# Dilated attention in a six-layer single-core kernel: the head norms' squares as high and low part, the key norms behind the next queries, and the group shares worked out over 128 rows

## The chip, the cores and the metric

One Trainium2 chip, one of its cores. The metric is the time of one execution on the device, in microseconds (us).

## The reference

A token stream of 512 positions by 1024 features goes through four layers (a mixer and a gated feed-forward each) and one more mixer. The third layer's mixer is dilated attention, and the change lies in it alone. It has three groups of 16 heads, each head 64 wide, with dilations 1, 4 and 16. Cut to what matters:

```python
qkv = (h @ w_qkv).reshape(b, s, 3, 3, 16, 64)
for g, (window, dil) in enumerate(((128, 1), (512, 4), (2048, 16))):
    q = head_rms_norm(qkv[:, :, g, 0], q_gain[g])      # each head's 64 numbers
    k = head_rms_norm(qkv[:, :, g, 1], k_gain[g])
    v = qkv[:, :, g, 2]
    o, l = dilated_group_attention(q, k, v, bias_g, dil, 64)   # softmax within the group; l = log of its sum
wts = softmax(stack(lses), axis=0)                     # the share of each group, per head and position
o = einsum('gbsh,gbshe->bshe', wts, stack(outs))
return o.reshape(b, s, 1024) @ w_o
```

## The kernel before

Bass code with one in-order program for each engine, written out by Python loops; every wait is on a semaphore count (`K.at(event)`). Features lie on partitions, the 512 positions on the free axis. A weight matrix comes in units of 128x2048 numbers (`raw`), which ScalarE rounds to fp32r (`wh`, `high`) and VectorE completes with the rest (`wl`, `low`). A product with a weight tile is three fp32r matmuls: high by high, high by low, low by high (`gemm`). Plain fp32 operands are used elsewhere; the trace shows an fp32 matmul as two records.

**The attention stage** (`attention_tensor` at L1845 and its sisters for the other engines) goes over three groups g, and in each over ten steps c. Step c of 0 to 7 makes the queries (j=0) and keys (j=1) of head pair c: 24 matmuls each, into a PSUM bank of the ring `K.gb` (four banks). The norm of each needs the sum of squares over a head's 64 rows: ScalarE squares the bank into `sq`, `head_tensor` (L1664) multiplies `sq` by a block matrix of ones (`K.bones`, in `cst`) in one fp32 matmul, and `head_scalar` (L1671) takes Ln and Exp of the result into `htf`. `head_vector` (L1680) multiplies the bank by gain and `htf` into `qk`. Step c also does the scores of pair c-1 (`scores_tensor`, L1690), and for pair c-2 the transposes of the probabilities `Pm` (`products_tensor`, L1766), their copies to SBUF (`PT`, `turned_out`: ScalarE the even ones, VectorE the odd ones), and the products with the values. The norms, transposes and scores share the ring `K.mb` of four banks: a bank is taken again only when its reader is done. For c of 2 to 7 the key norm's matmul stands behind the second transpose of `products_tensor`:

```python
        m.then_inc(*pe.up("T", t))
        if n == 1 and c + 2 < 8:
            head_tensor(K, pe, g, c + 2, 1)
```

Steps 8 and 9 have no projection of their own: they finish the last two pairs, and in groups 0 and 1 make the values of the next group. `mst` and `den` keep each row's maximum and sum of exponentials, 128 rows by group, block and head. Each pair's output goes through `os` to DRAM (`sA`).

**The mix** (`mix_tensor` at L1960 and its sisters) behind it has every engine wait for the end of the attention on all engines (`fence`, L237) and for the last two writes to `sA`. TensorE turns `mst` and `den` to 16 rows (heads) by 512 positions in 24 transposes; VectorE works out the three shares on those 16 rows, six copies and a chain of twelve operations of 512 columns and a reciprocal, with three Exp on ScalarE between; they end in `M`, which GpSimd has set to zero first (`mset`, L2081). Then, for each of 8 pairs c, three fp32 matmuls with a selection matrix `sel` spread a head's share over its 64 rows, VectorE and GpSimd multiply the three outputs `ol` (read back from `sA` by `mix_sync`, L2092, into three buffers) by them and add, ScalarE and GpSimd make the fp32r high and low parts (`omh`, `oml`), and TensorE's `take_in` multiplies them with the output weights.

## Time and profile before

| | us |
|---|---|
| median of 3 runs (lowest, highest) | 3106.11 (3103.87, 3107.86) |
| the profiled execution | 3106.0 |
| its span in the trace | 3104.2 |
| TensorE busy | 2840.2 (91%) |
| VectorE, ScalarE, GpSimd busy | 1560.2, 1092.7, 236.4 |
| mean granted clock of TensorE | 0.955 |

Busy time is summed over the span. The trace's matmuls are pipelined, so a record of 0.39 us may stand every 0.23 us; what a stream of matmuls costs is read from the starts. The granted clock is 1.00 at TensorE's full 2.4 GHz and 0.50 at 1.2 GHz. The attention stage's pair loops lie between 1200 and 1731 us of the span, the mix between 1731 and about 1830.

### The profile page before, as it was taken

The page shows a single profiled execution, that of the slowest core. Times are in us where ns is not written, and L with a number is a line of the kernel's source. Part 1 is how long each engine was busy: PE and PEld are TensorE (multiplying, and loading weights), DVE is VectorE, ACT ScalarE, POOL GpSimd, SP SyncE. Part 2 cuts the span into 40 slices and gives each one's busy share as a digit, 9 for nine tenths or more (in the row PEclk, how much of TensorE's full clock was granted, in tenths as well). Part 3 has the DMA queues.
Part 4 walks back from the last instruction along what each step waited for, and adds up shares of the span by engine and source line. Part 5 has one row for each costly group of instructions (what it writes and reads, how often), then busy time and mean ns, then how long its engine had stood idle before and what let it go on. Part 6 is the DMA issues. An engine that isn't in the chain of part 4 may idle for free.

```text
span 3104.2 us, 37866 instructions
## 1 busy us (share of the span) xinstructions
PE 2840.2 (91%) x15334; PEld 2271.0 (73%) x15334; DVE 1560.2 (50%) x2305; ACT 1092.7 (35%) x1672; POOL 236.4 (8%) x215
## 2 busy tenths in 40 slices
PE   5999997579999989989999699999799999888887
PEld 5787886467888867767777478888688888666665
DVE  5776663844434433553424554344554344544665
ACT  4332332353222223544536242122332122442342
...
GB/s 110 85 144 172 144 164 175 201 145 94 132 116 123 100 61 95 69 76 94 70 101 85 121 87 95 95 99 95 52 86 103 97 95 95 78 42 42 40 15 43
DMA packets 115135, 305.32 MB, mean 98 GB/s; under 512 B 28064, under 2 KB 73568, under 8 KB 86160
## 3 DMA queue, kind: packets, MB, share of 16 engines
...
q8 instruction: 120, 1.97, 0.3%
...
## 4 chain that ended last, share of the span: by engine, by line
PE 79%; DVE 8%; ACT 4%; issue 3%; POOL 1%; SPq 1%; DMA 0%; ACTq 0%; DVEq 0%; POOLq 0%
PE ps L94 78%; DVE s_ L121 2%; PE ps L99 1%; ACT htf_ L117 1%; ACT wh_ L117 1%; SPq L158 1%; DVE H_ L121 1%; DVE htf_ L135 1%; ACT hh_ L117 1%; ACT sq_ L117 0%; DVE R_ L121 0%; DVE ol_ L121 0%; DVE x_ L121 0%; ACT rs_ L117 0%; POOL hl_ L121 0%
## 5 line engine op out<-in xcount | busy, mean ns | idle before, releaser
L94 PE MATMUL ps<-hh_,wh_ 128*128 128x512 f32 x2184 | 872.9, 400 | 19.0 <-DVE hl_ L121 11.5
L94 PE MATMUL ps<-hl_,wh_ 128*128 128x512 f32 x2184 | 857.8, 393 | 0.0
L94 PE MATMUL ps<-hh_,wl_ 128*128 128x512 f32 x2184 | 857.2, 392 | 0.0
L121 DVE TENSOR_TENSOR wl_<-raw_,wh_ 128x2048 fp32r<-128x2048 f32 (+2 forms) x213 | 480.8, 2257 | 556.8 <-ACT wh_ L117 556.7
L117 ACT ACTIVATE wh_<-raw_ 128x2048 fp32r<-128x2048 f32 (+2 forms) x213 | 399.8, 1877 | 374.9 <-PE ps L94 356.7
L94 PEld LDWEIGHTS ps<-hh_,wh_ 128*128 128x128 f32 x2184 | 414.3, 190 | 121.7 <-issue 10.5
L94 PEld LDWEIGHTS ps<-hh_,wl_ 128*128 128x128 f32 x2184 | 414.4, 190 | 88.0
L94 PEld LDWEIGHTS ps<-hl_,wh_ 128*128 128x128 f32 x2184 | 415.0, 190 | 87.2 <-issue 3.5
L94 PE MATMUL ps<-ah_,wl_ 128*128 128x512 f32 x704 | 279.5, 397 | 0.0
L94 PE MATMUL ps<-ah_,wh_ 128*128 128x512 f32 x704 | 278.3, 395 | 0.0
L94 PE MATMUL ps<-al_,wh_ 128*128 128x512 f32 x704 | 277.7, 395 | 0.0
L117 ACT ACTIVATE sg_<-sg_ 128x512 f32<-128x512 f32 x88 | 55.7, 633 | 305.3 <-DVE sg_ L121 305.3
L94 PEld LDWEIGHTS ps<-al_,wh_ 128*128 128x128 f32 x704 | 132.1, 188 | 32.7
L94 PEld LDWEIGHTS ps<-ah_,wh_ 128*128 128x128 f32 x704 | 132.1, 188 | 32.5 <-issue 1.3
L94 PEld LDWEIGHTS ps<-ah_,wl_ 128*128 128x128 f32 x704 | 132.1, 188 | 31.5
L121 DVE TENSOR_TENSOR sg_<-sg_,ps 128x512 f32<-128x512 f32 x88 | 60.5, 688 | 171.2 <-PE ps L94 130.4
L117 ACT ACTIVATE ah_<-sg_ 128x512 fp32r<-128x512 f32 x88 | 55.7, 633 | 238.9 <-DVE sg_ L121 238.9
L121 DVE TENSOR_TENSOR x_<-x_,ps 128x512 f32<-128x512 f32 x104 | 71.2, 684 | 127.2 <-PE ps L94 127.2
L117 ACT ACTIVATE sq_<-x_ 128x512 f32<-128x512 f32 x70 | 44.2, 632 | 217.7 <-DVE x_ L121 209.7
L94 PE MATMUL ps<-wh_,hh_ 128*128 128x512 f32 (+2 forms) x272 | 104.3, 383 | 9.6 <-POOL hl_ L121 5.8
L94 PE MATMUL ps<-wl_,hh_ 128*128 128x512 f32 (+2 forms) x272 | 102.3, 376 | 0.0
L94 PE MATMUL ps<-wh_,hl_ 128*128 128x512 f32 (+2 forms) x272 | 102.2, 376 | 0.0
...
## 6 DMA issues: line engine op xcount, KB each, us to landing
...
```

The source lines that it names most:

```text
L94: return self.e.matmul(out, lhsT, rhs, start=start, stop=stop, skip_group_check=True)
L99: return self.e.transpose(out, a, ident)
L117: return self.e.activation(out, a, f, bias=bias, scale=scale)
L121: return Nothing() if self.e is None else self.e.tensor_tensor(out, a, b, op)
L135: return self.e.scalar_tensor_tensor(out=out, in0=a, scalar=s, in1=b, op0=op0, op1=op1)
L158: return Nothing() if self.e is None else self.e.dma_start(out, a)
```

## The change

- The squares are split by ScalarE into `sqh` (fp32r) and, by GpSimd, the rest `sql`; `head_tensor` multiplies each by an fp32r copy of the ones (`bonr`), two fp32r matmuls in the place of one of fp32. There is one `sqh` and one `sql` for both j, so each is written only when the matmul before has read it.
- The key norm of pair c-1 is taken between the query and key projections of step c; that of the last pair in `products` of step 7.
- Group 0's `mst` and `den` are brought into the other groups' order of positions at steps 3 and 5 of group 1 (`regroup`, 8 transposes each time, a copy each on ScalarE and VectorE).
- The shares are worked out before they are turned, over 128 rows by 64 columns a group: maxima at group 2's steps 1 and 8, one Exp in step 9, the rest in step 9 behind the last `PT` copy. Then 12 transposes turn them, ScalarE and VectorE split them into `Mh` and `Ml` (16 rows), and 48 fp32r matmuls replace the 24 of fp32. `M`, its memset and the 512 KB load of `sel` are gone; 16x16 of `sel` are loaded early and spread by VectorE.
- The fences before the mix no longer name the last writes to `sA`; the loads of pairs 6 and 7 wait for them.

```diff
 def head_tensor(K, pe, g, c, j):
     b = K.mb.take("n", g, c, j)
     pe.wait_ge(*K.after(pe, K.mb, "n", g, c, j))
-    pe.wait_ge(*K.at("a.sq", g, c, j))
-    pe.mm(b, K.bones, K.sq[j][:, :], True, True).then_inc(*pe.up("n", g, c, j))
+    A = K.att
+    pe.wait_ge(*K.at("a.ones"))
+    pe.wait_ge(*K.at("a.sqh", g, c, j))
+    pe.mm(b, A.ones[:, :], A.sqh[:, :], True, False)
+    pe.wait_ge(*K.at("a.sql", g, c, j))
+    pe.mm(b, A.ones[:, :], A.sql[:, :], False, True).then_inc(*pe.up("n", g, c, j))
+
+
+def squares_scalar(K, ac, g, c, j):
+
+    ac.wait_ge(*K.at("qk", g, c, j))
+    if c or g:
+        ac.wait_ge(*K.at("a.sql", *((g, c - 1) if c else (g - 1, 7)), j))
+    ac.act(K.sq[j][:, :], K.gb["qk", g, c, j], ACT.Square).then_inc(*ac.up())
+    if j:
+        ac.wait_ge(*K.at("n", g, c, 0))
+    elif c or g:
+        ac.wait_ge(*K.at("n", *((g, c - 1) if c else (g - 1, 7)), 1))
+    ac.wait_ge(*ac.now())
+    ac.act(K.att.sqh[:, :], K.sq[j][:, :], ACT.Copy).then_inc(*ac.up("a.sqh", g, c, j))
+
+
+def squares_gpsimd(K, po, g, c, j):
+    po.wait_ge(*K.at("a.sqh", g, c, j))
+    po.tt(K.att.sql[:, :], K.sq[j][:, :], K.att.sqh[:, :].bitcast(F32), ALU.subtract).then_inc(*po.up("a.sql", g, c, j))
 ...
         for y, (x, c0, nk, _) in enumerate(sub):
             m = pe.tr(b[0:nk, 128 * y:128 * y + 128], A.Pm[i][:, h, x, c0:c0 + nk], K.ident)
         m.then_inc(*pe.up("T", t))
-        if n == 1 and c + 2 < 8:
-            head_tensor(K, pe, g, c + 2, 1)
     pe.mark("a.T", g, c)
     for n in range(0, len(todo), 2):
         if scores is not None:
             scores_tensor(K, pe, g, scores, n // 2)
+        if n == 0 and c == 5:
+            head_tensor(K, pe, g, 7, 1)
         weigh(n)
     pe.mark("O", g, c)
 
@@ -1826,8 +1852,11 @@
     for n in range(len(turned_parts(g))):
         if turned_number(g, c, n) % 2 == 0:
             turned_out(K, ac, g, c, n)
-        if n == 1 and c + 2 < 8:
-            head_scalar(K, ac, g, c + 2, 1)
+    if c == 5:
+        head_scalar(K, ac, g, 7, 1)
+    if (g, c) == (2, 7):
+        ac.wait_ge(*K.at("m.e"))
+        ac.act(K.att.E[:, :, :], K.att.E[:, :, :], ACT.Exp).then_inc(*ac.up("m.x"))
     ac.wait_ge(*K.at("O", g, c))
     if 8 * g + c > 1:
         ac.wait_ge(*K.at("a.sA", 8 * g + c - 2))
@@ -1838,8 +1867,81 @@
     for n in range(len(turned_parts(g))):
         if turned_number(g, c, n) % 2:
             turned_out(K, dv, g, c, n)
-        if n == 1 and c + 2 < 8:
-            head_vector(K, dv, g, c + 2, 1)
+    if c == 5:
+        head_vector(K, dv, g, 7, 1)
+
 ...
+def regroup_tensor(K, pe, back):
+    A = K.att
+    for n, src in enumerate(statistics(K)):
+        b = K.mb.take("rg", back, n)
+        pe.wait_ge(*K.after(pe, K.mb, "rg", back, n))
+        if not back:
+            pe.wait_ge(*K.at("a.P", 0, 7, 1))
+            pe.wait_ge(*K.at("a.mx", 0, 7, 1))
+            for x in range(4):
+                m = pe.tr(b[0:16, 128 * x:128 * x + 128], src[:, 0, x, :], K.ident)
+        else:
+            pe.wait_ge(*K.at("out", "rg", 0, n))
+            for r in range(4):
+                m = pe.tr(b[:, 16 * r:16 * r + 16], A.turn[:, n, :].rearrange("p (i r) -> p r i", r=4)[:, r, :], K.ident[0:16, 0:16])
+        m.then_inc(*pe.up("rg", back, n))
+
+
 ...
+def shares_vector(K, dv, part):
+    A = K.att
+    mst, den = (t[:, :, :, :].rearrange("p g b x -> p g (b x)") for t in statistics(K))
+    E, F, Q = A.E, A.F, A.Q
+    if part == 0:
+        dv.wait_ge(*dv.now())
+        for n in range(2):
+            dv.wait_ge(*K.at("rg", 1, n))
+        dv.tt(Q[:, 0, :], mst[:, 0, :], mst[:, 1, :], ALU.max).then_inc(*dv.up())
+    elif part == 1:
+        dv.wait_ge(*dv.now())
+        dv.tt(Q[:, 0, :], Q[:, 0, :], mst[:, 2, :], ALU.max).then_inc(*dv.up())
+        dv.wait_ge(*dv.now())
+        dv.tt(E[:, :, :], mst, Q[:, 0:1, :].broadcast_to([128, 3, 64]), ALU.subtract).then_inc(*dv.up("m.e"))
+    else:
+        dv.wait_ge(*K.at("a.P", 2, 7, 1))
+        dv.wait_ge(*K.at("out", "rg", 1, 1))
+        dv.wait_ge(*K.at("m.x"))
+        dv.tt(F[:, :, :], E[:, :, :], den, ALU.mult).then_inc(*dv.up())
+        dv.wait_ge(*dv.now())
+        dv.tt(Q[:, 0, :], F[:, 0, :], F[:, 1, :], ALU.add).then_inc(*dv.up())
+        dv.wait_ge(*dv.now())
+        dv.tt(Q[:, 0, :], Q[:, 0, :], F[:, 2, :], ALU.add).then_inc(*dv.up())
+        dv.wait_ge(*dv.now())
+        dv.recip(Q[:, 1, :], Q[:, 0, :]).then_inc(*dv.up())
+        dv.wait_ge(*dv.now())
+        dv.tt(F[:, :, :], E[:, :, :], Q[:, 1:2, :].broadcast_to([128, 3, 64]), ALU.mult).then_inc(*dv.up("m.F"))
+        dv.wait_ge(*K.at("m.sel"))
+        dv.cp(K.mix.sel[:, :, :].rearrange("p c (n x) -> p (c n) x", n=2),
+              A.sel0[:, :].rearrange("p (n x) -> p n x", x=1).broadcast_to([16, 16, 64])).then_inc(*dv.up("m.selr"))
 ...
                     pe.wait_ge(*K.after(pe, K.gb, "qk", g, c, j))
                     gemm(K, pe, K.gb["qk", g, c, j], rhs, 8)
                     pe.mark("qk", g, c, j)
+                    if c and not j:
+                        head_tensor(K, pe, g, c - 1, 1)
                 head_tensor(K, pe, g, c, 0)
             if c > 1:
                 products_tensor(K, pe, g, c - 2, c - 1 if c < 9 else None)
+            if g == 1 and c in (3, 5):
+                regroup_tensor(K, pe, c // 4)
             if c > 7 and g < 2:
                 values_tensor(K, pe, g + 1, c - 8)
-            if c < 2:
-                head_tensor(K, pe, g, c, 1)
             if c == 1:
                 scores_tensor(K, pe, g, 0)
 ...
             if c < 8:
                 for j in range(2):
                     highs(K, ac, 8)
-                    ac.wait_ge(*K.at("qk", g, c, j))
-                    if c or g:
-                        ac.wait_ge(*K.at("n", *((g, c - 1) if c else (g - 1, 7)), j))
-                    ac.act(K.sq[j][:, :], K.gb["qk", g, c, j], ACT.Square).then_inc(*ac.up("a.sq", g, c, j))
+                    squares_scalar(K, ac, g, c, j)
+                    if c and not j:
+                        head_scalar(K, ac, g, c - 1, 1)
                 head_scalar(K, ac, g, c, 0)
 ...
+            if g == 2 and c in (1, 8, 9):
+                shares_vector(K, dv, c - 7 if c > 7 else 0)
 ...
     A = K.mix
-    for n, (src, name) in enumerate(((K.att.mst, "M"), (K.att.den, "dn"))):
-        for g in range(3):
-            b = K.mb.take("m.t", n, g)
-            pe.wait_ge(*K.after(pe, K.mb, "m.t", n, g))
-            for x in range(4):
-                m = pe.tr(b[0:16, 128 * x:128 * x + 128], src[:, g, x, :], K.ident)
-            m.then_inc(*pe.up("m.t", n, g))
+    for g in (2, 0, 1):
+        b = K.mb.take("m.t", g)
+        pe.wait_ge(*K.after(pe, K.mb, "m.t", g))
+        pe.wait_ge(*K.at("m.F"))
+        for x in range(4):
+            m = pe.tr(b[0:16, 128 * x:128 * x + 128], K.att.F[:, g, 16 * x:16 * x + 16], K.ident)
+        m.then_inc(*pe.up("m.t", g))
 ...
-            pe.wait_ge(*K.at("m.F"))
-            pe.wait_ge(*K.at("m.sel"))
-            pe.mm(b, A.sel[:, c, :], A.M[:, g, :], True, True).then_inc(*pe.up("m.b", c, g))
+            pe.wait_ge(*K.at("out", "m.t", g))
+            pe.wait_ge(*K.at("m.selr"))
+            pe.mm(b, A.sel[:, c, :], A.Mh[:, g, :], True, False)
+            pe.mm(b, A.sel[:, c, :], A.Ml[:, g, :], False, True).then_inc(*pe.up("m.b", c, g))
 ...
+def shares_high(K, ac, g):
+
+    ac.wait_ge(*K.at("m.t", g))
+    ac.act(natural(1, K.mix.Mh[:, g, :], False), natural(1, K.mb["m.t", g][0:16, :], True), ACT.Copy).then_inc(*ac.up("m.Mh", g))
+
+
+def shares_low(K, dv, g):
+
+    dv.wait_ge(*K.at("m.Mh", g))
+    dv.tt(natural(1, K.mix.Ml[:, g, :], False), natural(1, K.mb["m.t", g][0:16, :], True),
+          natural(1, K.mix.Mh[:, g, :].bitcast(F32), False), ALU.subtract).then_inc(*dv.up("out", "m.t", g))
+
+
 ...
     A = K.mix
-    M, E, Q, dn = A.M[0:16, :, :], A.E, A.Q, A.dn
-    dv.wait_ge(*K.at("m.z"))
-    for n, dst in enumerate((M, dn)):
-        for g in range(3):
-            dv.wait_ge(*K.at("m.t", n, g))
-            dv.cp(natural(g, dst[:, g, :], False), natural(g, K.mb["m.t", n, g][0:16, :], True)).then_inc(*dv.up("out", "m.t", n, g))
-    dv.wait_ge(*dv.now())
-    dv.tt(Q[:, 0, :], M[:, 0, :], M[:, 1, :], ALU.max).then_inc(*dv.up())
-    dv.wait_ge(*dv.now())
-    dv.tt(Q[:, 0, :], Q[:, 0, :], M[:, 2, :], ALU.max).then_inc(*dv.up())
-    dv.wait_ge(*dv.now())
-    for g in range(3):
-        dv.tt(E[:, g, :], M[:, g, :], Q[:, 0, :], ALU.subtract).then_inc(*dv.up("m.e", g))
-    for g in range(3):
-        dv.wait_ge(*K.at("m.x", g))
-        dv.tt(E[:, g, :], M[:, g, :], dn[:, g, :], ALU.mult).then_inc(*dv.up())
-    dv.wait_ge(*dv.now())
-    dv.tt(Q[:, 1, :], E[:, 0, :], E[:, 1, :], ALU.add).then_inc(*dv.up())
-    dv.wait_ge(*dv.now())
-    dv.tt(Q[:, 1, :], Q[:, 1, :], E[:, 2, :], ALU.add).then_inc(*dv.up())
-    dv.wait_ge(*dv.now())
-    dv.recip(Q[:, 0, :], Q[:, 1, :]).then_inc(*dv.up())
-    dv.wait_ge(*dv.now())
-    for g in range(3):
-        dv.tt(M[:, g, :], M[:, g, :], Q[:, 0, :], ALU.mult).then_inc(*dv.up())
-    dv.mark("m.F")
+    for g in (2, 0, 1):
+        shares_low(K, dv, g)
 ...
 
 def mix_sync(K, sp):
     A, d = K.mix, K.d
-    sp.dma(A.sel[:, :, :], d["sel"]).then_inc(*K.lane("sel").up("m.sel"))
-    sp.wait_ge(*K.at("a.sA", 22))
-    sp.wait_ge(*K.at("a.sA", 23))
     for c in range(8):
         if c > 2:
             sp.wait_ge(*K.at("m.l", c - 3))
+        if c > 5:
+            sp.wait_ge(*K.at("a.sA", 16 + c))
         for g in range(3):
```

ScalarE's order in group 1, one step (`sq0`, `sq1` the squares of queries and keys, `htf` Ln and Exp of a norm, `PT` a transposed block, `os` the output). Before:

```order
L117 ACTIVATE sq0_<-ps0 128x512 [waits scalar_done,tensor_done]
L117 ACTIVATE sq1_<-ps1 128x512 [waits scalar_done,tensor_done]
L117 ACTIVATE htf0_<-ps6,eps_ 128x512 [waits scalar_done,tensor_done]
L117 ACTIVATE htf0_<-htf0_ 128x512 [waits scalar_done]
L117 ACTIVATE PT0_<-ps7 128x512 [waits tensor_done]
L117 ACTIVATE htf1_<-ps5,eps_ 128x512 [waits scalar_done,tensor_done]
L117 ACTIVATE htf1_<-htf1_ 128x512 [waits scalar_done]
L117 ACTIVATE os0_<-ps2 128x512 [waits sA0,tensor_done]
```

and in the changed kernel:

```order
L117 ACTIVATE sq0_<-ps0 128x512 [waits scalar_done,gpsimd_done,tensor_done]
L117 ACTIVATE sqh_<-sq0_ 128x512 [waits scalar_done,tensor_done]
L117 ACTIVATE htf1_<-ps7,eps_ 128x512
L117 ACTIVATE htf1_<-htf1_ 128x512 [waits scalar_done]
L117 ACTIVATE sq1_<-ps1 128x512 [waits gpsimd_done,tensor_done]
L117 ACTIVATE sqh_<-sq1_ 128x512 [waits scalar_done,tensor_done]
L117 ACTIVATE htf0_<-ps4,eps_ 128x512
L117 ACTIVATE htf0_<-htf0_ 128x512 [waits scalar_done]
L117 ACTIVATE PT0_<-ps5 128x512 [waits tensor_done]
L117 ACTIVATE os0_<-ps2 128x512 [waits scalar_done,sA0,tensor_done]
```

The keys' Ln and Exp (`htf1`) went from behind the transposed block to ahead of the keys' squares, and a rounding to `sqh` now stands between the keys' squares and the queries' Ln.

TensorE's order in the changed kernel, where a step's key projection (`ps3`) begins and ends:

```order
L94 MATMUL ps5<-sqh_,bonr_ 128x512 [waits scalar_done]
L94 MATMUL ps5<-sql_,bonr_ 128x512 [waits gpsimd_done]
L94 MATMUL ps3<-hh_,wh0_ 128x512
L94 MATMUL ps3<-hl_,wh0_ 128x512
L94 MATMUL ps3<-hh_,wl0_ 128x512
...
L94 MATMUL ps6<-sqh_,bonr_ 128x512 [waits scalar_done]
L94 MATMUL ps6<-sql_,bonr_ 128x512 [waits gpsimd_done]
L99 MATMUL ps7<-cst_,Pm0_ 128x128 [waits vector_done]
```

The pair into `ps5` is the norm of the step before's keys, the pair into `ps6` that of this step's queries; before, only the latter stood here, as one fp32 matmul.

VectorE's order at the end of the attention, from the last block's statistics to the mix, before:

```order
L128 TENSOR_SCALAR nmx_<-nmx_ 128x4 [waits vector_done]
L139 COPY PT3_<-ps7 128x512 [waits tensor_done]
L139 COPY M_<-ps4 16x512 [waits sA0,sA1,gpsimd_done,vector_done,tensor_done,scalar_done]
L139 COPY M_<-ps5 16x512 [waits tensor_done]
```

and in the changed kernel (`V_` here holds the shares in work):

```order
L128 TENSOR_SCALAR nmx_<-nmx_ 128x4 [waits vector_done]
L121 TENSOR_TENSOR V_<-V_,mst_ 128x64 [waits vector_done]
L121 TENSOR_TENSOR V_<-mst_,V_ 128x192 [waits vector_done]
L139 COPY PT3_<-ps7 128x512 [waits tensor_done]
L121 TENSOR_TENSOR V_<-V_,den_ 128x192 [waits vector_done,scalar_done]
L121 TENSOR_TENSOR V_<-V_ 128x64 [waits vector_done] x2
L151 RECIPROCAL V_<-V_ 128x64 [waits vector_done]
L121 TENSOR_TENSOR V_<-V_ 128x192 [waits vector_done]
L139 CAST sel_<-sel0_ 16x1024 [waits sel]
L121 TENSOR_TENSOR Ml_<-ps4,Mh_ 16x512 [waits gpsimd_done,vector_done,scalar_done,tensor_done]
```

The chain of operations that stood behind the fence stands ahead of it, on 64 or 192 columns; behind the fence three subtractions are left.

## Rows read from the trace of the kernel before

**Rows 1.** The page, the chain that ended last, by engine.

```profile
PE 79%; DVE 8%; ACT 4%; issue 3%; POOL 1%; SPq 1%; DMA 0%; ACTq 0%; DVEq 0%; POOLq 0%
```

**Rows 2.** Timeline of one step of group 1: start us, us, engine, operation.

```profile
1463.27 0.39 PE L94 MATMUL ps<-hh_,wl_ 128*128 128x512 f32 x1
1463.50 1.02 PE L94 MATMUL ps<-sq_,cst_ 128*128 128x512 f32 x2
1463.70 0.60 ACT L117 ACTIVATE sq_<-ps 128x512 f32<-128x512 f32 x1 [4.01 <-PE ps L94]
1464.36 1.04 PE L99 MATMUL ps<-cst_,Pm_ 128*128 128x128 f32 x8
1464.56 0.69 ACT L117 ACTIVATE htf_<-ps,eps_ 128x512 f32<-128x512 f32 x1 [0.26 <-PE ps L94]
1465.23 1.02 PE L94 MATMUL ps<-sq_,cst_ 128*128 128x512 f32 x2
1465.81 0.58 ACT L117 ACTIVATE PT_<-ps 128x512 f32<-128x512 f32 x1
1465.94 0.75 DVE L135 SCALAR_TENSOR_TENSOR qk_<-ps,gq_,htf_ 128x512 f32<-128x512 f32 x1 [4.41 <-ACT htf_ L117]
1466.54 1.16 PE L94 MATMUL ps<-qk_ 64*128 64x128 f32 x16 [0.28 <-ACT PT_ L117]
1466.61 0.68 DVE L139 COPY PT_<-ps 128x512 f32<-128x512 f32 x1
1467.63 1.09 PE L94 MATMUL ps<-PT_,V_ 128*64 128x128 f32 x16
```

**Rows 3.** The chain, group 1 from its first step: start us, us, what.

```profile
1385.62 62.74 PE ps L94 x298
1450.37 14.16 PE ps L94 x82
```

**Rows 4.** The chain, group 0's step 7.

```profile
1330.11 0.70 ACT htf_ L117
...
1332.95 3.21 PE ps L94 x32
...
1336.16 0.68 DVE Pm_ L121
```

**Rows 5.** The chain, group 2's steps 7 and 8.

```profile
1711.08 0.70 ACT htf_ L117
...
1718.40 1.11 PE ps L99 x4
```

**Rows 6.** GpSimd's operations of the mix by tile: ns min/median/max, first and last start.

```profile
L121 POOL TENSOR_TENSOR ol_<-ol_,sq_ x8: 1266/1509/2868, 1754.0 to 1791.8; 128x512 f32<-128x512 f32 x8
```

**Rows 7.** Timeline from the last products to the first use of the shares.

```profile
1728.87 1.97 PE L94 MATMUL ps<-PT_,V_ 128*64 128x128 f32 x16 [0.87 <-DVE PT_ L139]
...
1731.94 0.37 SPq L158 DMA_DIRECT2D sel_<-in_sel  x1
...
1733.69 4.30 SPq L158 DMA_DIRECT2D ol_<-sA  x9
...
1745.62 3.34 DVE L151 RECIPROCAL Q__<-Q__ 16x512 f32<-16x512 f32 x1
...
1756.64 0.69 DVE L121 TENSOR_TENSOR ol_<-ol_,ps 128x512 f32<-128x512 f32 x1 [0.96 <-PE ps L94]
```

**Rows 8.** The tile of the outputs read back, its transfers.

```profile
DMA to landing us min/median/max: 2.6/3.8/5.9
```

**Rows 9.** The chain in the mix, VectorE's last sum of two pairs in succession.

```profile
1779.02 0.70 DVE ol_ L121
...
1783.52 0.70 DVE ol_ L121
```

**Rows 10.** Windows behind TensorE's waits: the number behind GpSimd's busy time is the clock.

```profile
1364.00:1366.00 2.00, 2.00 (x7) 1.58 (x6) 1.97 (x7) 0.00 (x0) 0.00 (x0) 0.55 0.00 0
...
2729.00:2731.00 2.00, 0.42 (x5) 0.42 (x5) 2.00 (x4) 1.38 (x3) 0.00 (x0) 1.00 0.42 78
```

More of the change, by code:

```diff
@@ L155, in mset, with dma @@
         return Nothing() if self.e is None else self.e.memset(out, v)
-    def dma(self, out, a):
-        return Nothing() if self.e is None else self.e.dma_start(out, a)
+    def dma(self, out, a, single=False):
+        if self.e is None:
+            return Nothing()
+        return self.e.dma_start(out, a, allow_slow_non_contiguous=True) if single else self.e.dma_start(out, a)
 class Lane:
@@ new lines, in regroup_scalar, with regroup_vector @@
+def regroup_scalar(K, ac, back):
+    ac.wait_ge(*K.at("rg", back, 1))
+    if not back:
+        ac.wait_ge(*K.at("O", 0, 7))
+        ac.act(K.att.turn[:, 1, :], K.mb["rg", 0, 1][0:16, :], ACT.Copy).then_inc(*ac.up("out", "rg", 0, 1))
+    else:
+        ac.act(K.att.den[:, 0, :, :].rearrange("p b x -> p (b x)"), K.mb["rg", 1, 1][:, 0:64], ACT.Copy).then_inc(*ac.up("out", "rg", 1, 1))
+def regroup_vector(K, dv, back):
+    dv.wait_ge(*K.at("rg", back, 0))
+    if not back:
+        dv.wait_ge(*K.at("O", 0, 7))
+        dv.cp(K.att.turn[:, 0, :], K.mb["rg", 0, 0][0:16, :]).then_inc(*dv.up("out", "rg", 0, 0))
+    else:
+        dv.cp(K.att.mst[:, 0, :, :].rearrange("p b x -> p (b x)"), K.mb["rg", 1, 0][:, 0:64]).then_inc(*dv.up("out", "rg", 1, 0))
@@ L1872, in attention_scalar @@
     A = K.att
+    ac.act(A.ones[:, :], K.bones, ACT.Copy).then_inc(*ac.up("a.ones"))
     rstd_scalar(K, ac, 4)
@@ L1891, in attention_scalar @@
                 products_scalar(K, ac, g, c - 2)
+            if g == 1 and c in (3, 5):
+                regroup_scalar(K, ac, c // 4)
             if c == 8 and g == 0:
                 residues_scalar(K, ac, range(4, 8))
-            if c < 2:
-                head_scalar(K, ac, g, c, 1)
             if 0 < c < 9:
@@ L1914, in attention_vector @@
                 lows(K, dv, 16)
+                if c:
+                    head_vector(K, dv, g, c - 1, 1)
                 head_vector(K, dv, g, c, 0)
@@ L1919, in attention_vector @@
                 products_vector(K, dv, g, c - 2)
+            if g == 1 and c in (3, 5):
+                regroup_vector(K, dv, c // 4)
             if c == 8 and g == 0:
                 residues_vector(K, dv, g_, range(4, 8))
-            if c < 2:
-                head_vector(K, dv, g, c, 1)
             if 0 < c < 9:
@@ L1933, in attention_gpsimd @@
         norm_gpsimd(K, po, 4, k)
-    residues_gpsimd(K, po)
+    for g in range(3):
+        for c in range(8):
+            for j in range(2):
+                squares_gpsimd(K, po, g, c, j)
+        if g == 0:
+            residues_gpsimd(K, po)
     po.mark("end", "po", "attend")
@@ L1940, in attention_sync @@
     sp.dma(A.gq[:, :], d["qkg"]).then_inc(*K.lane("qkg").up("a.gq0"))
+    sp.dma(A.sel0[:, :].rearrange("p (c n) -> p c n", n=2), d["sel"][0:16, :, 0:128:64], single=True).then_inc(*K.lane("sel").up("m.sel"))
     for g in range(3):
@@ L2002, in mix_tensor @@
     pe.mark("end", "pe", "mix")
+def shares_high(K, ac, g):
[5 more added lines that the diff above has]
+          natural(1, K.mix.Mh[:, g, :].bitcast(F32), False), ALU.subtract).then_inc(*dv.up("out", "m.t", g))
 def mix_scalar(K, ac, s, g_):
     A = K.mix
-    for g in range(3):
-        ac.wait_ge(*K.at("m.e", g))
-        ac.act(A.M[0:16, g, :], A.E[:, g, :], ACT.Exp).then_inc(*ac.up("m.x", g))
+    for g in (2, 0, 1):
+        shares_high(K, ac, g)
     for c in range(8):
@@ L2030, in mix_vector @@
     A = K.mix
[L2031 to L2056 removed]
+    for g in (2, 0, 1):
+        shares_low(K, dv, g)
     for c in range(8):
@@ L3547, in memory @@
         A.gq = K.sb(st, "gq", [128, 6])
+        A.sqh, A.sql = (K.sb(st, n, [128, 512], R32) for n in ("sqh", "sql"))
+        A.sel0 = K.sb(st, "sel0", [16, 16])
+        A.ones = K.sb(st, "bonr", [128, 128], R32)
         with ExitStack() as s2:
             A.V = K.sb(s2, "V", [128, 5, 1024])
+            A.E, A.F, A.Q = (A.V[:, 4, a:b].rearrange("p (g x) -> p g x", x=64) for a, b in ((0, 192), (192, 384), (384, 512)))
+            A.turn = A.V[0:16, 4, :].rearrange("p (n x) -> p n x", n=2)
             A.qk = [[K.sb(s2, f"qk{i}{j}", [128, 512]) for j in range(2)] for i in range(2)]
@@ L3558, in memory @@
             M.ml = K.sb(s2, "oml", [128, 8, 512], R32)
-            M.sel = K.sb(s2, "sel", [128, 8, 128])
-            M.M = K.sb(s2, "M", [128, 3, 512])
-            M.E = K.sb(s2, "E_", [16, 3, 512])
-            M.Q = K.sb(s2, "Q_", [16, 2, 512])
-            M.dn = K.sb(s2, "dn", [16, 3, 512])
             M.ol = [K.sb(s2, f"ol{i}", [128, 3, 512]) for i in range(3)]
+            K.sb(s2, "kept", [128, 1536])
+            M.Mh, M.Ml = (K.sb(s2, n, [16, 3, 512], R32) for n in ("Mh", "Ml"))
+            M.sel = K.sb(s2, "sel", [16, 8, 128], R32)
     for f in (2, 3):
@@ L3658, in scalar @@
     attention_scalar(K, ac)
-    fence(K, ac, "attend", ("a.sA", 22), ("a.sA", 23))
+    fence(K, ac, "attend")
     mix_scalar(K, ac, 5, 6)
@@ L3692, in vector @@
     attention_vector(K, dv, 2)
-    fence(K, dv, "attend", ("a.sA", 22), ("a.sA", 23))
+    fence(K, dv, "attend")
     mix_vector(K, dv, 5, 6)
@@ L3723, in gpsimd @@
     attention_gpsimd(K, po)
-    fence(K, po, "attend", ("a.sA", 22), ("a.sA", 23))
+    fence(K, po, "attend")
     mix_gpsimd(K, po)
```

5 lines of the change are left out of this document (3 added, 2 removed).

## The prediction

> **What bounds the kernel now.** I read the chain of waits first, then the timeline of the attention and of the mix. The chain runs over TensorE for 79% of the span [rows 1], so what counts is what TensorE does or waits for, and on which engine it waits.
>
> In one step of group 1 [rows 2], let G be the end of the last projection matmul, 1463.27 + 0.39 = 1463.66. All offsets below are from G. The query norm's fp32 matmul runs till 1464.53 (0.87), ScalarE's Ln starts at 1464.56 (0.90), Exp follows, then `PT` at 1465.81. TensorE meanwhile does eight transposes (0.87) and the key norm (its row at 1465.23, 0.87). It still waits 0.28 for ScalarE's `PT` before the scores at 1466.54, and starts the products with the values at 1467.63 (3.97). So in a middle step of group 1 or 2 the key norm's 0.87 lies wholly beside ScalarE's chain Ln, Exp, `PT`: taking it away there gives nothing. The matmul after G begins 0.23 after the one before it, so an fp32r matmul costs 0.2275 in a stream, a pair 0.455, and an fp32 one 0.865 (1464.36 - 1463.50).
>
> At the first steps of group 1 it is otherwise: one piece of TensorE work of 62.74 us, with no wait in it, leads into the first such step [rows 3]. At the last steps the chain leaves TensorE: key norm's Ln, VectorE's multiply, adds and maxima, Exp, transposes, in group 0 [rows 4] and in group 2 [rows 5].
>
> **The change, part by part.**
>
> *A middle step, groups 1 and 2.* New in the stream: the key norm of the pair before, 0.455, between two projections, where TensorE has no wait that could hide it. The query norm behind G takes 0.455 for 0.865. But ScalarE now rounds the keys' squares before it takes Ln. It squares at 0.04 to 0.64 [rows 2], waits for the query norm (done at 0.48), and rounds at 0.67. A rounding of 128x512 has no row of its own in this step; the bounds are 0.58 (`PT`) and 0.69 (Ln), and I take 0.63. Operations without a tie between them overlap by 0.1 on ScalarE, so Ln starts at 1.20, not 0.90. From it follow Exp at 1.92, VectorE's `qk` at 2.58 and its `PT` at 3.25 to 3.94 (each as far behind Ln as in [rows 2]). TensorE's scores need only Ln's bank and are done at 3.05; the products wait for VectorE's `PT` and start at 4.08, where they started at 3.97. So a step becomes 0.455 + 0.11 = 0.57 longer, although it has less fp32 work. There are five such steps in each group (c = 2 to 6): 2.8 us a group.
>
> *A middle step, group 0.* The scores wait there for VectorE's `PT` in both kernels [rows 4], 2.84 behind Ln. Ln comes 0.30 later, so the step is 0.455 + 0.30 = 0.76 longer, five times: 3.8.
>
> *The first two steps.* In groups 1 and 2 they lose four fp32 norms and get three pairs of fp32r (the fourth is in c = 2, counted): 4 x 0.865 - 3 x 0.455 = 2.1 shorter a group, since TensorE has no wait there [rows 3]. In group 0 some of it turns into a wait for Ln; I take 1.9.
>
> *Step 7 and what follows.* The last key norm now stands behind the scores. In groups 1 and 2 they end at 3.05, the norm at 3.5, and its Ln starts at 3.6. Before, it started at 2.62 (1711.08 in [rows 5], G there being 1708.46 by the same count). The chain through the last transposes (1718.40) starts from it, so it is 0.95 later, with the 0.455 of pair 6: 1.4. In group 0 the scores' first part starts at 4.04 and takes 0.85, the norm ends at 5.35, Ln, Exp and the multiply (0.70 + 0.63 + 0.75) bring it to 7.5. Then come two adds and two maxima of 192 columns, about 0.3 each by 192/512 of the 0.68 row, so the add that stood at 1336.16 [rows 4], 6.95 after G = 1329.21, stands at 8.65: 1.7 later, 2.2 with pair 6.
>
> *Regrouping, group 1.* Sixteen transposes in steps that are TensorE's own. Eight take 0.87 [rows 2]; the second eight have 16 columns and may cost little. Bounds 0.9 and 1.75; I take 1.5. Their copies delay VectorE's adds by some 2.4 and the Exps behind them, which have most of a step of spare time; cost nothing.
>
> *GpSimd's 48 subtractions.* A query's `sql` is needed at the next G, about 3.2 after its `sqh` in group 0 and more in the others. GpSimd's like operation takes 1.27 to 2.87, median 1.51 [rows 6]. I take it as hidden, by 0.3 at worst. The Trainium skill (GPSIMD Engine Reference, Specifications) says that GpSimd shares its way to SBUF with VectorE and loses time beside VectorE operations with two SBUF inputs, of which the weights' subtraction is one. By that rule the 2.87 would be the normal case here and the spare time 0.3, which still leaves the sum as it is; it is what gives rival C its chance.
>
> Sum of the attention: group 0, -1.9 + 3.8 + 2.2 = +4.1; group 1, -2.1 + 2.8 + 1.4 + 1.5 = +3.6; group 2, -2.1 + 2.8 + 1.4 = +2.1. Together +9.8.
>
> *The shares.* Before, the last products end at 1730.85 [rows 7]. Then come transposes, GpSimd's memset, VectorE's copies and its chain on 16 rows (the reciprocal alone 3.34) and the spreading matmuls at the slow clock; VectorE's second multiply of pair 0 starts at 1756.64, 25.8 later. The change does the chain on 128 rows ahead of that. The shares are five operations of 64 or 192 columns behind the last `PT` copy, which ended about 0.14 ahead of 1728.87: by columns the reciprocal is 3.34 x 64/512 = 0.42 and the others 0.2 to 0.3, some 1.6 in all, done before 1730.85. Transposes at the slow clock (0.2 each), split on ScalarE and VectorE, and three pairs of matmuls make the first shares ready by about 1735.8. That is not the last thing to arrive. SyncE passes its fence as before, near 1731.94 (VectorE's spread of `sel`, about 1.3, ends at 1731.6), and then issues `ol` at once, not at 1733.69: the third load at 0.48 each (4.30/9) goes out at 1732.9. It lands 2.6 to 5.9 later [rows 8], median 3.8: 1736.7. The two multiplies start at 1736.7 and 1737.4. Against 1756.64 that is 19.3 less; by the bounds of the landing 17.2 to 20.5.
>
> *The rest of the mix.* A pair takes 4.50 on GpSimd, VectorE and ScalarE [rows 9]; TensorE's 12 + 6 matmuls of 0.2275 are less than that, as its work was nearly before. So 24 x 0.41 of matmul time saved there is worth nothing. Cover: the 4.50 cycle; without it, up to 9.8 more would show.
>
> Total: +9.8 - 19.3 = -9.5. The profiled execution took 3106.0 with a span of 3104.2, and the median of the runs is 3106.11, so the forecast is **3096.6**.
>
> **Rivals.**
>
> *A, the attention loses nothing.* The chains have slack I don't see, and added norms are paid by those removed. For it: 48 x 0.41 = 19.7 of TensorE time really is gone. Against: the 0.28 wait in [rows 2], which shows that TensorE already waits. With the attention at 0 the time is 3086.8; with all 19.7 gained, 3067.
>
> *B, slower: the clock.* New waits of about 0.6 and 1.0 in each step of groups 1 and 2, and of 1.8 in group 0, could bring the clock to 1.2 GHz for the start of the next projection. For it: in a window behind a wait of 1.94 the clock was 0.55; against it: behind a thinner stretch, busy 0.42 of 2 us, it was 1.00 [rows 10]. The price is that of some eight matmuls at twice 0.2275, about 1.6 a step. If all 22 steps paid it, +35: 3132. It decides from ten steps on. The Trainium skill (TensorE: Matmul & The Clock Gate, "A second HAM failure mode: psum-queue depth-cycling") describes such short idles between groups of matmuls as enough to make the clock change back and forth; this kernel's middle steps ran at 1.00 with a 0.28 wait, which doesn't test it.
>
> *C, no change to speak of.* `sql` comes late in group 0 by about a us a step (+7), or the mix starts on loads that land at 5.9 and runs TensorE at the slow clock through its first pairs (+2 to +6). Either leaves 3100 to 3104. That the shares' part doesn't take effect is excluded by the order.
>
> **How the numbers follow.** The forecast's own case has 0.58, with a range of 3092 to 3100 from the landing (2.1 and 1.2), the regrouping (0.6) and steps with a little more or less wait (22 x 0.1). A has 0.14, C 0.17, B 0.11. The range to 8 in 10 is 3087 to 3105: it takes in A at 0, and C. A measurement can tell 0.2%, 6.2 us, from no change. Faster by more means under 3099.9: my case but for its upper edge (0.54), and A (0.14): 0.68. Within: C and that edge, 0.21. Slower: B, 0.11.
>
> **What the profile would show.** Right: the products of a middle step of group 1 start 4.1 after G behind VectorE's `PT`, Ln 1.2 after G, a step of 16.7 us for 16.17; the clock stays at 1.00 in these steps; VectorE's multiply of pair 0 stands some 6.5 behind the last products, released by a load. Wrong: Ln right behind the query norm (A), matmuls 0.43 apart at a step's start (B), TensorE waiting for GpSimd's `sql` (C), or a gap of over 10 us at the mix's start.

## The result: slightly slower, and where the time went

| | before | changed |
|---|---|---|
| median of 20 runs, us | 3107.05 (3100.37 to 3109.95) | 3112.57 (3103.05 to 3122.54) |
| ratio, 95% interval | 1 | 1.0018 (1.0011 to 1.0025) |
| profiled execution, us | 3106.0 | 3114.4 |
| its span, us, and mean granted clock | 3104.2, 0.955 | 3112.6, 0.951 |

The changed kernel is 5.5 us slower, where 9.5 less was forecast, and its runs lie twice as far apart. To see where, I cut both profiled executions at the same instructions (ScalarE's Square behind each query projection, the last products, GpSimd's last low part, the next norm's sum of squares) and put the forecast's terms beside them. The two right columns are repetitions and repairs that come below.

| difference to before, us | forecast | changed | changed, profiled again | changed and mended in three places |
|---|---|---|---|---|
| attention, group 0 | +4.1 | +12.1 | +13.7 | +4.8 |
| attention, group 1 | +3.6 | +5.3 | +7.0 | +5.2 |
| attention, group 2 to its last products | +2.1 | +3.5 | +3.5 | +3.4 |
| last products to the mix's last low part | -19.3 | -19.6 | -18.8 | -19.7 |
| from there to the next norm | 0 | +2.4 | +2.0 | 0.0 |
| sum | -9.5 | +3.7 | +7.4 | -6.3 |

The first profile is 4.8 us behind already at the first Square; 3.3 of this lie ahead of every changed instruction, and 1.5 in the values' projection, where the same instructions run at the slow clock for a stretch. From the next norm to the end both kernels take 1273.9 us in these two executions. That is chance in part: the second profile of the changed kernel takes 1270.2 there, and the profiles of the versions below 1266.0 to 1274.5, with the same instructions. What follows is therefore read between the cuts, where a step repeats to some hundredths, and not from spans. So the mix gained what was forecast; the attention lost twice its term, most of it in group 0; and a loss that no term had stands behind the mix.

**The mechanism of a step is as forecast.** The timeline of the changed kernel, a step of group 1 without regrouping, to be read beside [rows 2] (start us, us, engine, operation):

```profile
1514.24 0.40 PE L94 MATMUL ps<-sqh_,bonr_ 128*128 128x512 f32 x1
1514.44 0.60 ACT L117 ACTIVATE sq_<-ps 128x512 f32<-128x512 f32 x1 [3.36 <-PE ps L94]
1514.47 0.40 PE L94 MATMUL ps<-sql_,bonr_ 128*128 128x512 f32 x1
1514.71 1.03 PE L99 MATMUL ps<-cst_,Pm_ 128*128 128x128 f32 x8
1515.13 0.63 ACT L117 ACTIVATE sqh_<-sq_ 128x512 fp32r<-128x512 f32 x1
1515.66 0.67 ACT L117 ACTIVATE htf_<-ps,eps_ 128x512 f32<-128x512 f32 x1
1516.48 1.16 PE L94 MATMUL ps<-qk_ 64*128 64x128 f32 x16 [0.73 <-ACT htf_ L117]
1517.70 0.68 DVE L139 COPY PT_<-ps 128x512 f32<-128x512 f32 x1
1518.53 1.09 PE L94 MATMUL ps<-PT_,V_ 128*64 128x128 f32 x16 [0.89 <-DVE PT_ L139]
```

The end of the last projection matmul, G, is at 1514.40. Ln starts 1.26 behind it (forecast 1.20), held up by the rounding, and the products 4.13 (4.08), held up by VectorE's `PT`; such a step takes 16.83 us (16.74). A step is measured here and below from ScalarE's Square of one step's keys to that of the next.

**Group 0 is where it went wrong.** First the wait ahead of the scores in step 3 of group 0 before the change; then the same step of the changed kernel, TensorE's rows behind the transposes, and the windows over them (the number behind GpSimd's busy time is the granted clock):

```profile
1256.22 0.92 PE L94 MATMUL ps<-qk_ 64*128 64x192 f32 x8 [0.25 <-DVE PT_ L139]
```

```profile
1262.31 0.92 PE L94 MATMUL ps<-qk_ 64*128 64x192 f32 x8 [1.53 <-DVE PT_ L139]
1263.16 1.98 PE L94 MATMUL ps<-PT_,V_ 64*64 64x128 f32 x16
1265.07 1.98 PE L94 MATMUL ps<-qk_ 64*128 64x256 f32 x8
```

```profile
1260.00:1262.00 2.00, 0.66 (x4) 0.39 (x4) 1.23 (x3) 1.77 (x6) 0.85 (x1) 1.00 0.02 4
1262.00:1264.00 2.00, 1.69 (x16) 1.26 (x18) 1.59 (x6) 0.00 (x0) 0.00 (x0) 0.85 0.00 0
1264.00:1266.00 2.00, 2.00 (x16) 1.58 (x14) 0.38 (x2) 0.00 (x0) 0.00 (x0) 0.50 0.04 8
```

TensorE waits 0.21 for a bank, ahead of the last four transposes, and then 1.53 for the scores' inputs; before, the keys' norm stood among the transposes and 0.25 of the wait was left. Behind the wait the clock is at its lower level, 1.2 GHz: the same sixteen products take 1.98 us, in other steps 1.24. Steps 2 to 6 of group 0 take 21.13, 21.67, 20.38, 20.11 and 23.21 us (19.17 to 19.21 before). An undisturbed one takes 0.94 more than before (forecast 0.76); steps 3 and 6 have 1.6 and 3.1 on top, with the slow clock behind the wait. From step 7 to the first Square of group 1, the passage, it takes 88.6 for 86.1; there too the clock is at 0.50 behind the wait of 1.53.

Step 2 is long for another reason, in the timeline of the changed kernel:

```profile
1234.72 2.29 DVE L121 TENSOR_TENSOR wl_<-raw_,wh_ 128x2048 fp32r<-128x2048 f32 x1 [3.85 <-ACT wh_ L117]
1235.97 2.18 POOL L121 TENSOR_TENSOR sql_<-sq_,sqh_ 128x512 fp32r<-128x512 f32 x1 [11.32 <-ACT sqh_ L117]
1238.21 0.51 PE L94 MATMUL ps<-sql_,bonr_ 128*128 128x512 f32 x1 [1.22 <-POOL sql_ L121]
```

GpSimd's subtraction takes 2.18 us beside VectorE's subtraction of the weights, and TensorE waits 1.22 for it, in step 2 of groups 1 and 2 about 0.5. The queries' subtraction is that long in every step from 2 on (2.07 to 2.21; the keys' takes 1.27 to 1.30), but only in step 2 is it late: there it starts 1.1 us ahead of G, in step 3 3.1. The Trainium skill (GPSIMD Engine Reference, Specifications) has the reason as a shared way to SBUF; its sign agrees, its size comes from these rows.

**The mix starts as forecast, and ends with a new loss.** The start, in the timeline of the changed kernel, beside [rows 7]:

```profile
1754.52 1.98 PE L94 MATMUL ps<-PT_,V_ 128*64 128x128 f32 x16 [0.88 <-DVE PT_ L139]
1755.19 0.55 DVE L151 RECIPROCAL V_<-V_ 128x64 f32<-128x64 f32 x1
1757.61 4.35 SPq L161 DMA_DIRECT2D ol_<-sA  x9
1762.05 1.28 DVE L121 TENSOR_TENSOR ol_<-ol_,ps 128x512 f32<-128x512 f32 x2 [1.82 <-DMA ol_<-sA]
```

The reciprocal takes 0.55 for 3.34, the loads go out at 1757.61, and VectorE's two multiplies wait for a load. The second starts at 1762.7, 6.2 behind the last products, for 25.8 before and 6.5 forecast. The end, TensorE ahead of the last pair, first before, then changed:

```profile
1798.23 0.50 PE L94 MATMUL ps<-omh_,wh_ 128*128 128x512 f32 x1 [2.16 <-POOL oml_ L121]
1798.57 0.39 PE L94 MATMUL ps<-oml_,wh_ 128*128 128x512 f32 x1
1798.80 0.40 PE L94 MATMUL ps<-omh_,wl_ 128*128 128x512 f32 x1
```

```profile
1804.29 0.79 PE L94 MATMUL ps<-omh_,wh_ 128*128 128x512 f32 x1 [4.39 <-POOL oml_ L121]
1804.88 0.63 PE L94 MATMUL ps<-oml_,wh_ 128*128 128x512 f32 x1
1805.31 0.63 PE L94 MATMUL ps<-omh_,wl_ 128*128 128x512 f32 x1
```

With the cheaper spreading matmuls TensorE is done earlier and waits 4.39 for 2.16; behind that wait the matmuls start 0.43 apart instead of 0.23, for twelve of them: 12 x 0.2 = 2.4 us.

So the theory (theory 1 in the expectations) is this: the change makes TensorE's waits longer, in group 0 by a wait ahead of the scores and in the mix by saved work, and the granted clock falls behind them; GpSimd is late three times; the rest is stream time, near the forecast.

### The profile page after: what moved, and what is told of

Same layout as the page of the kernel before. It is cut to its first block and busy times, and to the rows that moved or that the text cites. A ratio compares the mean times of both kernels' runs of the same rounds, so it can differ in the third digit from the quotient of the medians.

```text
span 3112.6 us, 38014 instructions
## 1 busy us (share of the span) xinstructions
PE 2832.3 (91%) x15338; PEld 2286.3 (73%) x15338; DVE 1550.8 (50%) x2299; ACT 1120.9 (36%) x1724; POOL 312.2 (10%) x262
## 5 line engine op out<-in xcount | busy, mean ns | idle before, releaser
L121 POOL TENSOR_TENSOR sql_<-sq_,sqh_ 128x512 fp32r<-128x512 f32 x48 | 77.1, 1607 | 474.9 <-ACT sqh_ L117 474.9
L135 DVE SCALAR_TENSOR_TENSOR qk_<-ps,gq_,htf_ 128x512 f32<-128x512 f32 x48 | 36.0, 751 | 134.0 <-ACT htf_ L117 133.9
```

Of the source, the lines that this page charges most:

```text
L121: return Nothing() if self.e is None else self.e.tensor_tensor(out, a, b, op)
L135: return self.e.scalar_tensor_tensor(out=out, in0=a, scalar=s, in1=b, op0=op0, op1=op1)
```

## The experiments

All ratios are to the kernel before, run on the same chip.

**The changed kernel again.** 

> The changed kernel once more, as the other side of the comparison with the filled one. Theory 1: about 3112, runs spread over 10 to 20 us, and in the profile the granted clock at 0.5 behind the wait in some steps of group 0, not the same ones as in the first profile (2 and 7) by need. Rival (the longer steps are in the program): the same steps are long, 21.7 and 23.2 us.

3112.97 us (3105.2 to 3116.9, 11 runs), ratio 1.0015 (1.0006 to 1.0024). The profile has the steps of group 0 at 21.11, 21.67, 20.38, 20.11, 23.21: the same two are slow. Theory 1 left the place open, and here the rival's figures came true: the place of the fall is fixed by the program's timing, at least in these two executions. A new fall stands in step 5 of group 1, a step with regrouping (19.46 us for 17.87), and the passage takes 90.3. This run alone can't tell the clock from late inputs; the next one does.

**Filling the wait of group 0.** In `products_tensor`, behind the transposes:

```diff
+    if g == 0 and c < 6:
+        for _ in range(5):
+            pe.mm(O, A.ones[:, :], K.hh[:, 0, :], True, True)
```

`O` is overwritten by the products. 

> The changed kernel with five matmuls of 0.2275 us more (1.14 us, a product that is overwritten) in each of six steps of group 0, behind the last transposes, where TensorE waits 1.5 us for the scores' inputs. Theory 1 (the wait lets the granted clock fall to half in one to three of these steps of an execution, at 1.6 to 3.3 us each): no such fall, steps 3 to 7 of group 0 at 20.1 us, the time 3 to 8 us below the changed kernel's 3112.6 and its runs closer together. Rival (the longer steps of group 0 come from late inputs, with the clock only following): the same 3112, with as wide a spread.

3103.65 us (3102.2 to 3111.1, 11 runs), ratio 0.9992 (0.9983 to 1.0001): 9.3 us below the changed kernel run beside it, with 30 matmuls more. The kernel filled in group 0, the same place in its timeline, and a window over its wait:

```profile
1256.36 1.40 PE L94 MATMUL ps<-hh_,bonr_ 128*128 128x512 f32 x5
1258.14 0.92 PE L94 MATMUL ps<-qk_ 64*128 64x192 f32 x8 [0.38 <-DVE PT_ L139]
1258.99 1.24 PE L94 MATMUL ps<-PT_,V_ 64*64 64x128 f32 x16
```

```profile
1257.00:1259.00 2.00, 1.62 (x14) 0.94 (x12) 1.65 (x5) 0.62 (x3) 0.00 (x0) 1.00 0.01 4
```

The scores start as far behind the transposes as without the filling (2.2 us behind the start of the last four), so nothing arrives sooner; only the clock is different. Steps 3 to 6 take 20.14, 20.41, 20.10, 20.10, and in step 7 the clock is at 1.00 behind the wait, too. The theory of late inputs falls. Of the 9.3, 4.6 are in steps 3 and 6. The passage is 1.6 to 3.3 shorter (87.0), but how much of that is the filling stays open: two versions below with no slow step in group 0 have passages of 88.9 and 89.2. The rest has no place in the changed part: the two profiled executions differ by 2.7 us already ahead of the first Square.

**The shares alone.** The attention's norms and their order from the kernel before, all else from the changed one. 

> The shares' part alone (regrouping, shares over 128 rows, new start of the mix) with the attention's norms and their order as before. Theory 1 (the mix gained what was forecast, and the attention lost about 19.5 us instead of 9.8): -19.3 at the mix, +1.5 to +1.8 for the regrouping, so about 3089, 17.5 us below before. Rival (the mix gained less, about 10, and the attention lost what was forecast): about 3098 to 3099. By either, the steps of group 0 are 19.17 us as before.

3091.02 us (3088.0 to 3092.8, 5 runs), ratio 0.9946 (0.9934 to 0.9958). Theory 1 holds, though its 3089 left out the loss behind the mix, which is here in full (+2.4): the shares bring 16 us, and the two steps with regrouping are 0.76 and 1.04 longer (16.94 and 17.22 for 16.18), 1.8 together, where the forecast had 1.5. The norms' part of the change therefore costs 22 us.

**The move alone, and the split alone.** First both norms as one fp32 matmul in the changed order. 

> The changed kernel with both norms as single fp32 matmuls, in the changed order: the keys' norm between the next projections. It isolates the move. Theory 1: the keys' norm costs its whole 0.865 us in the stream in each of five middle steps of each group (13 us), the last one comes later in step 7 (about 1.2 a group), Ln stands at 0.90 behind G as before, so the wait ahead of the scores in group 0 is about 1 us and the clock seldom falls: 3091 + 13 + 4 = 3108, up to 3112 if it does fall. Rival (the move is nearly free, the split is what costs, by ScalarE's rounding and GpSimd's lateness): 3091 to 3096.

3105.86 us (3098.7 to 3110.0, 12 runs), ratio 0.9994 (0.9984 to 1.0004): 15 above the shares alone. A middle step takes 20.17 in group 0 (+0.99) and 16.88 in the others (+0.70), all alike, so the clock holds in the steps; the passage takes 88.9. The rival, by which the move is nearly free, falls. Then the split in the order of before. 

> Both norms by high and low part, but in the order of before: the keys' norm behind the first eight transposes. It isolates the split. Theory 1: the keys' low part is ready only 2.6 us behind G (Square 0.6, rounding 0.63, GpSimd 1.27), while TensorE gets there at 1.3: TensorE waits 1.2 us in a middle step of group 0 and its later parts shift by about 1.5, 0.3 in the others, and about 2 us in each of the first two steps of a group: 8 + 3 + 12 over the 3084 of the version with the queries' split alone, about 3107, with more falls of the clock. Rival (GpSimd's part is hidden in either order): 3080 to 3085.

3110.86 us (3105.6 to 3116.6, 12 runs), ratio 1.0015 (1.0007 to 1.0024), nearly 20 above the shares alone and 27 above the version below in which only the queries are split. In this version's timeline of group 0, and in its list of waits (engine, releaser: us, times, longest):

```profile
1302.05 1.29 POOL L123 TENSOR_TENSOR sql_<-sq_,sqh_ 128x512 fp32r<-128x512 f32 x1 [1.85 <-ACT sqh_ L119]
1302.11 0.47 PE L96 MATMUL ps<-sqh_,bonr_ 128*128 128x512 f32 x1 [0.17 <-ACT sqh_ L119]
1303.39 0.50 PE L96 MATMUL ps<-sql_,bonr_ 128*128 128x512 f32 x1 [0.80 <-POOL sql_ L123]
```

```profile
PE ps L96 <- POOL sql_ L123: 21.3, 25, 1.7
```

The split needs ScalarE and GpSimd one after the other before TensorE may go on. In the first two steps of groups 1 and 2, three stretches at the slow clock are added to the waits, with steps up to 3.1 longer than before. So the split of the keys costs 27 in the old place, and the move costs 15 by itself. Of the versions run, those with the keys' norm as it was are the fastest.

**The queries' split alone.** Keys as before; the queries' squares, whose rounding and subtraction fall into the next projection, are split. 

> As the one before, but the queries' norms (j = 0) by high and low part, in their old place; keys' norms in fp32 in their old place behind the first eight transposes. Theory 1: what hurt was the keys' norm in the stream and the keys' rounding ahead of Ln; the queries' split alone brings Ln from 0.90 to about 0.67 behind G (ScalarE's Square of the keys then ends last), 0.2 us a step in 16 steps and 0.41 in the two first of each group: 5.7 less, about 3084. Rival (any split norm costs, since GpSimd's subtraction or ScalarE's rounding is late somewhere): 3089 to 3093.

3084.11 us (3080.1 to 3086.6, 5 runs), ratio 0.9926 (0.9913 to 0.9940): 6.9 below the shares alone (forecast 5.7). In its timeline Ln starts 0.54 behind G (1497.34), sooner than my 0.67: it starts 0.50 behind the start of the Square, whose row is 0.60 long:

```profile
1497.38 0.60 ACT L119 ACTIVATE sq_<-ps 128x512 f32<-128x512 f32 x1 [3.36 <-PE ps L96]
1497.42 0.39 PE L96 MATMUL ps<-sql_,bonr_ 128*128 128x512 f32 x1
1497.65 1.03 PE L101 MATMUL ps<-cst_,Pm_ 128*128 128x128 f32 x8
1497.88 0.68 ACT L119 ACTIVATE htf_<-ps,eps_ 128x512 f32<-128x512 f32 x1
```

Middle steps take 18.80 and 15.80 for 19.17 and 16.17. Step 2 of group 0 takes 20.75: TensorE waits 1.69 for `sql` there.

**The query early in step 2.** To the last version, in `attention_scalar`:

```diff
-                    highs(K, ac, 8)
+                    if (c, j) != (2, 0):
+                        highs(K, ac, 8)
                     squares_scalar(K, ac, g, c, j)
+                    if (c, j) == (2, 0):
+                        highs(K, ac, 8)
```

> The version with the queries' split alone, and in step 2 of each group ScalarE squares and rounds the query ahead of the weights' rounding (1.90 us), so that GpSimd's subtraction doesn't fall beside VectorE's subtraction of the weights (2.2 us instead of 1.27) and isn't late. Theory 1: TensorE's wait of 1.69 us for GpSimd in step 2 of group 0 goes, and 0.5 in the others: 2.7 us below 3084.1, about 3081.5. Rival (the weights come late instead and take it back): 3084 or more.

3078.27 us (3077.9 to 3086.0, 4 runs), ratio 0.9906 (0.9892 to 0.9921). Its timeline, of the slowest of the four runs:

```profile
1235.00 1.30 POOL L123 TENSOR_TENSOR sql_<-sq_,sqh_ 128x512 fp32r<-128x512 f32 x1 [15.58 <-ACT sqh_ L119]
1236.76 2.29 DVE L123 TENSOR_TENSOR wl_<-raw_,wh_ 128x2048 fp32r<-128x2048 f32 x1 [5.00 <-ACT wh_ L119]
1237.23 0.39 PE L96 MATMUL ps<-sql_,bonr_ 128*128 128x512 f32 x1
```

GpSimd takes 1.30 again, the wait is gone, and the step takes 18.81. The steps account for 3 us, near the 2.7 expected; the other half of the 5.8 is within the runs' scatter (run again, this version took 3081.67).

**The keys' rounding late.** The changed kernel with ScalarE's rounding of the keys' squares behind its `PT` copies. 

> The changed kernel with ScalarE's rounding of the keys' squares put behind its PT copies (in steps 0 and 1 behind Ln and Exp), where nothing waits for it; step 7 as it was. Theory 1: Ln starts 0.67 behind G for 1.26, middle steps are 0.6 us shorter in all three groups (9 us), the wait ahead of the scores in group 0 falls to 0.9 and the granted clock holds (4.6 us): 3099 to 3103. Rival (the clock falls anyway, or ScalarE's later work, Exp and the weights' rounding, takes the 0.6 back): 3107 to 3112.

3096.01 us (3095.6 to 3098.5, 5 runs), ratio 0.9966 (0.9954 to 0.9978), even less than expected. Its timeline, group 1:

```profile
1501.88 0.60 ACT L119 ACTIVATE sq_<-ps 128x512 f32<-128x512 f32 x1 [3.36 <-PE ps L96]
1502.37 0.68 ACT L119 ACTIVATE htf_<-ps,eps_ 128x512 f32<-128x512 f32 x1
1504.10 0.62 ACT L119 ACTIVATE sqh_<-sq_ 128x512 fp32r<-128x512 f32 x1
```

Ln stands 0.49 behind the Square, not 1.22. Middle steps take 19.39 and 16.10, 0.7 less each, and no step of group 0 is at the slow clock. One of group 1 is: step 5, with regrouping, takes 18.77, where the changed kernel's second profile had its fall, too. One instruction of 0.63 us in the wrong place on ScalarE cost the changed kernel about 16 us, part of it through the clock.

**Filling the mix, and mending all three places.** Before the last pair's products in `mix_tensor`:

```diff
     take_in(6)
+    b = K.mb.take("fill")
+    pe.wait_ge(*K.after(pe, K.mb, "fill"))
+    for _ in range(12):
+        m = pe.mm(b, K.att.ones[:, :], A.mh[:, 0, :], True, True)
+    m.then_inc(*pe.up("out", "fill"))
     take_in(7)
```

> The version with the queries' split alone and the early query in step 2, with twelve matmuls more (2.7 us of TensorE, a product that nobody reads) in the mix, before the products of the last pair, where TensorE now waits 4.4 us for GpSimd's last low part (2.2 before the change). Theory 1 (the work that the shares' split saves on TensorE in the mix leaves a longer wait, behind which the granted clock is half for the next twelve matmuls, 2.4 us): the matmuls behind the wait are 0.23 apart again, 2.4 us less, about 3076. Rival (the clock is half there for the time of the wait only, or the added matmuls delay the last products): no change, 3078, or more.

> The version with the queries' split alone and the early query in step 2 once more, as the other side of the comparison with the one whose mix is filled: 3078, with four runs so far between 3077.9 and 3086.

> The changed kernel with the three places mended that the forecast had missed: five matmuls more in the wait of group 0's steps, the query early in step 2, twelve matmuls more in the mix. Theory 1 (these three make up the miss): 3103.7 of the version filled in group 0 alone, less 1.2 + 0.5 + 0.5 for the query in step 2 and 2.4 for the mix: 3099, near the 3096.6 that was forecast; the rest are the regrouping, 0.3 over its term, and middle steps of group 0 that are 0.2 longer than their term. Rival (there is another cause as large): 3103 or more.

Filled: 3079.54 us (3075.9 to 3082.6, 4 runs), ratio 0.9904 (0.9891 to 0.9918); not filled, beside it: 3081.67 (3080.0 to 3083.2, 4 runs), ratio 0.9911 (0.9898 to 0.9925). The runs alone don't settle 2 us, the trace does. The filled one:

```profile
1769.69 2.88 PE L96 MATMUL ps<-omh_,bonr_ 128*128 128x512 f32 x12
1774.25 0.50 PE L96 MATMUL ps<-omh_,wh_ 128*128 128x512 f32 x1 [1.68 <-POOL oml_ L123]
1774.59 0.39 PE L96 MATMUL ps<-oml_,wh_ 128*128 128x512 f32 x1
1774.82 0.40 PE L96 MATMUL ps<-omh_,wl_ 128*128 128x512 f32 x1
```

The matmuls are 0.23 apart, and from the last low part to the next norm it takes 33.3 us, as before (33.4); the version not filled takes 34.9 (35.7 in its first profile).

The changed kernel mended in all three places: 3099.96 us (3096.7 to 3104.5, 6 runs), ratio 0.9976 (0.9960 to 0.9992), expected 3099. These last three versions ran on another chip than the ones above, and there the kernel before took 3109.67; the ratio is the fairer figure. The steps 2 to 6 of its group 0 are all 20.1, and its column in the table above is within 1.6 us of each of the forecast's terms. With these three causes taken out, the forecast's sum holds but for 3 us: -6.3 for -9.5.

**What beats both:** the shares' part with the queries' split alone and the early query in step 2, 3078 to 3082 us, 0.9% below the kernel before; the mix filled is at least no worse.

## Why the prediction was wrong

The forecast was 9.5 us less; it came out 5.5 more. Most of the miss lies in one term, the middle steps of group 0 (+3.8), which took a new wait of TensorE at its length and left out the clock behind it; two smaller steps failed beside it, GpSimd's lateness at nothing and the mix's saved work at nothing. In the order of the forecast's terms:

*The mix start* (-19.3) was right in size and in mechanism: -19.6, the last thing to arrive is a load, 6.2 against 6.5.

*A middle step, groups 1 and 2* (+0.57): right, +0.67 with the wait named. *The first two steps* of groups 1 and 2 (-2.1): up to the keys' Square of step 2 it is 1.7 shorter, and that has pair 1's norm in it, 0.455, which the forecast counts in step 2; so 2.2, right. In group 0 the same stretch is 1.1 shorter, so 1.5 for the forecast's 1.9. *Regrouping* (1.5): 1.8. *Step 7 and what follows* (+1.4 in groups 1 and 2): 1.4 from step 7's Square on, and with pair 6's 0.455, which the forecast's 1.4 has in it, 1.8.

*A middle step, group 0* (+0.76): the term was 0.94 in itself, but the step that failed is the sentence that prices it by length alone. I had counted the new wait of 1.8 there, and under rival B I had the price of a fall, 1.6 us, about right: the two steps cost 1.6 and 3.1. What was wrong is that B was all or nothing (22 steps at +35, deciding from ten on), and its place. The clock falls in group 0, where the waits are longest, right behind the wait, in the scores and products, and not at the next projection: in two of the five steps and in step 7. I should have added to the main case a fall or two there. Which step it would be, no rule of mine gives: step 4 waits longer (0.49 and 1.54) than step 3 (0.21 and 1.53) and keeps the clock. The steps of groups 1 and 2, with 0.73 and 0.89, kept it in both profiles but for one.

*GpSimd's subtractions* ("hidden, by 0.3 at worst"): I had worked the spare time out for a middle step. Step 2 is the first in which ScalarE's Exps and the weights' rounding stand ahead of the query's Square, and TensorE comes to the norm sooner than later on, since step 1 has no products (15.1 us from step 1's keys to step 2's, 20.1 in later steps of group 0): 1.22 late in group 0, 0.5 in the two others. A length of 2.87 beside VectorE stood in [rows 6]; what was wrong was the due time, in one step in eight. It is rival C's sign, at 2.1 us for all three groups and not 7.

*The rest of the mix* ("24 x 0.41 of matmul time saved there is worth nothing"): it was worth less than nothing, +2.4. The cover that I named, the 4.50 us cycle, ends at the last pair; there the saved work turned into a longer wait at the clock's cost.

The sum, of the first profile: 4.7 from the clock in group 0's steps and about 1.6 in its passage (3.3 in the second profile, and less sure), 2.1 from `sql`, 2.4 behind the mix, 2 to 3 from terms a little too small. That is the 13.2 by which the table's sum misses (+3.7 for -9.5). By the medians the miss is 15.0 (+5.5 for -9.5; 3112.6 for 3096.6); the 1.8 between the two is within the scatter of code that the change leaves alone. Two of the three causes had the same root, a wait of TensorE that grows, and the one rival that priced it right was given all or nothing.
